# A real-part Fourier transform computed on folded halves, with one rotation table and one weight tile built or loaded at another place

## Chip, cores, metric

The kernel runs on one core of a Trainium2 chip. The time is device microseconds (us) of one execution; several executions are made and their median is quoted.

## What is computed

The program computes two transformer-like blocks over 1,024 positions of width 1,024. The change lies in the mixer of the first block. There a projection of the normalised input gives u (384 columns, a state-space mixer), f (256 columns, a Fourier mixer) and q, k, v (windowed attention). The Fourier mixer and the recurrence of the state-space mixer, cut to what matters:

```python
def fourier_mixer(f, w_fft):            # f: (1, 1024, 256), 4 heads of 64
    ff = f.astype(jnp.float32).reshape(bsz, seq, FFT_HEADS, HEAD_DIM)
    mixed = jnp.fft.fft2(ff, axes=(1, 3), norm='ortho').real.astype(f.dtype)
    return jnp.einsum('bshd,hde->bshe', mixed, w_fft).reshape(bsz, seq, FFT_WIDTH)
...
    lam_bar = jnp.exp(lam * dt)         # complex, 2 directions x 24 groups x 64 states
    _, h_dir = lax.associative_scan(_scan_combine, (a, bu), reverse=rev, axis=1)
```

Only the real part of the two-dimensional transform is kept. With A = f times the cosine matrix of the head dimension and B = f times minus the sine matrix (both already multiplied by `w_fft`), the result over positions is cos(2 pi s t / 1024) A plus sin(2 pi s t / 1024) B.

## The kernel before

Everything in this part of the program is written out by hand: each engine has its own list of instructions, semaphores join them, and the order in which an engine's instructions are written is the order in which it runs them. The transfers spoken of here are all issued from one queue, SP's.

**Projection.** Ten units of 128 output columns (`win_units`, lines 168 to 171): units 0 and 1 give f, 2 to 4 give u, 5 to 7 give q, 8 k, 9 v. For unit n, SP loads 512 KB of weights into `win_raw[n % 2]` (`load_unit`), ScalarE (ACT) rounds them to `win_upper` (line 2074), VectorE (DVE) subtracts to get `win_lower` (`split`, line 2296) and TensorE (PE) runs 48 matmuls of 512 columns (`unit_step`, line 2423). ACT then copies the unit from PSUM (line 2078, `z_ready`). PE's unit n waits for `split(n)` on DVE; ACT's `split(n)` waits for the end of unit n - 2; SP's load of unit n waits for `split(n - 2)` on DVE.

**The Toeplitz tile.** Between the loads of units 3 and 4, SP also writes the convolution taps to DRAM (15 transfers, lines 2007 and 2009), waits for them, and reads them back in shifted order into `toep` (8 transfers of 192 KB, line 2012). `toep` is first used by PE after the attention (line 359).

**The mixer's own order.** PE: the product of the head-dimension matrices with `w_fft` (line 251); the head-dimension stage on f, 8 position tiles with 256 moving columns per pair of heads (line 258), copied by ACT into `f_mixed` (line 393); transposes of u (line 267), copied by DVE into `u_rows` (line 457); transposes of `u_rows` (line 275), copied by ACT into `u_chunk` (line 396); transposes of v (line 280); then the transform over positions (line 289): 8 position tiles x cosine and sine x 2 pairs x 2 halves of the output = 64 fp32 matmuls of 512 columns into four PSUM banks, with 16 loads of 512 KB of the transform matrix through four buffers (line 238). ACT copies the four banks into `yc_t` (line 402, `yf_ready`). Only then PE goes on: a loop over 8 blocks with six items of attention each, beginning with `states` (line 305) and `scores` (line 314), while DVE does row maxima, rotation and scans.

**The rotation tables.** `turns(d)` on DVE builds, for each of the two directions, a 128 x 2 x 12 x 128 table of powers by seven doublings. A doubling of width w works on pieces of `step` of the 12 pairs, each piece being four multiplies, a wait, two adds and a wait (lines 477 to 483). Before, both tables are built after the six copies of `u_rows` and after PE's transposes of them (`uc_turned`, 6); the piece is at most 384 elements.

An fp32 matmul on PE shows as two records in the trace, so 64 matmuls are 128 records; a transpose and a matmul of the rounded operands (line 2423) show as one.

## Time and profile before

| | |
|---|---|
| runs of the kernel before | 3650.12, 3654.16, 3656.3 us; median 3654.16 |
| span of the profiled execution | 3651.0 us, 37524 instructions |
| PE busy | 3376.1 us (92%) |
| DVE busy | 1487.4 us (41%) |
| ACT busy | 1020.5 us (28%) |
| GpSimd (POOL) busy | 217.6 us (6%) |
| mean granted TensorE clock | 0.948 of full |
| chain that ended last, by engine | PE 80%, DVE 10%, issue 4%, ACT 4%, ACTq 1% |
| of it line 2423 (projection) and line 289 (transform over positions) | 2% and 2% |

The span runs from the first to the last instruction of one profiled execution. Its own device time is not given apart from the three runs above, so the table sets the span beside the median of the runs: 3.2 us lie between them. Times in the trace are counted from the start of the span. The stage in question lies between 160 and 370 us.

### The profile page before, as it was taken

The page shows a single profiled execution, that of the slowest core. Times are in us where ns is not written, and L with a number is a line of the kernel's source. Part 1 is how long each engine was busy: PE and PEld are TensorE (multiplying, and loading weights), DVE is VectorE, ACT ScalarE, POOL GpSimd, SP SyncE. Part 2 cuts the span into 40 slices and gives each one's busy share as a digit, 9 for nine tenths or more (in the row PEclk, how much of TensorE's full clock was granted, in tenths as well). Part 3 has the DMA queues.
Part 4 walks back from the last instruction along what each step waited for, and adds up shares of the span by engine and source line. Part 5 has one row for each costly group of instructions (what it writes and reads, how often), then busy time and mean ns, then how long its engine had stood idle before and what let it go on. Part 6 is the DMA issues. An engine that isn't in the chain of part 4 may idle for free.

```text
span 3651.0 us, 37524 instructions
## 1 busy us (share of the span) xinstructions
PE 3376.1 (92%) x14497; PEld 2602.1 (71%) x14497; DVE 1487.4 (41%) x2617; ACT 1020.5 (28%) x1475; POOL 217.6 (6%) x251
## 2 busy tenths in 40 slices
PE   6999888979999999999999998967788899999997
PEld 2575456768888788788888886656345688888885
DVE  6523541453433434411112354699642711111355
ACT  1211223343323223312112232314443322111231
POOL 4100110000000000000000000113330000000000
PEclk9899658989999999999999999888899999999998
DMA  8233000421111134311111342111002311111242
GB/s 276 93 57 107 1 7 24 142 66 47 48 50 46 58 98 140 117 48 46 52 46 52 98 140 97 36 35 39 1 1 98 115 52 46 52 46 46 92 141 100
DMA packets 245610, 260.35 MB, mean 71 GB/s; under 512 B 25680, under 2 KB 187464, under 8 KB 245396
## 3 DMA queue, kind: packets, MB, share of 16 engines
q1 hardware_dynamic: 235736, 253.05, 22.2%
q10 hardware_dynamic: 9788, 6.16, 0.6%
q8 instruction: 53, 0.87, 0.1%
q14 instruction: 33, 0.27, 0.0%
HBM read 237.55 MB, written 21.34 MB: 71 GB/s over the span
## 4 chain that ended last, share of the span: by engine, by line
PE 80%; DVE 10%; issue 4%; ACT 4%; ACTq 1%; DMA 0%; SPq 0%; DVEq 0%; POOL 0%
PE psum L925 39%; PE psum L780 24%; PE psum L2394 2%; PE psum L2423 2%; PE psum L1645 2%; DVE count_junk L1848 2%; PE psum L289 2%; PE psum L314 1%; PE psum L1545 1%; PE psum L333 1%; PE psum L1625 1%; PE psum L362 1%; DVE p L1913 1%; ACT probs L410 1%; PE psum L1635 1%
## 5 line engine op out<-in xcount | busy, mean ns | idle before, releaser
L925 PE MATMUL psum<-x_hi,split_hi 128*128 128x512 f32 x2112 | 662.1, 391 | 15.1 <-DVE x_lo L1197 15.1
L925 PE MATMUL psum<-x_lo,split_hi 128*128 128x512 f32 x2112 | 660.6, 390 | 0.0
L925 PE MATMUL psum<-x_hi,split_lo 128*128 128x512 f32 x2112 | 660.5, 390 | 0.0
L925 PEld LDWEIGHTS psum<-x_hi,split_hi 128*128 128x128 f32 x2112 | 398.3, 189 | 99.9 <-DVE x_lo L1197 17.0
L925 PEld LDWEIGHTS psum<-x_lo,split_hi 128*128 128x128 f32 x2112 | 398.4, 189 | 82.9
L925 PEld LDWEIGHTS psum<-x_hi,split_lo 128*128 128x128 f32 x2112 | 398.0, 188 | 82.9
L780 PE MATMUL psum<-split_hi,src_hi 128*128 128x512 f32 x1312 | 407.0, 392 | 19.6 <-DVE split_lo L750 12.4
L780 PE MATMUL psum<-split_lo,src_hi 128*128 128x512 f32 x1312 | 405.4, 390 | 0.0
L780 PE MATMUL psum<-split_hi,src_lo 128*128 128x512 f32 x1312 | 405.4, 390 | 0.0
L831 DVE TENSOR_TENSOR split_lo<-raw,split_hi 128x1024 fp32r<-128x1024 f32 x132 | 160.9, 1221 | 564.7 <-ACT split_hi L827 564.7
L827 ACT CAST split_hi<-raw 128x1024 fp32r<-128x1024 f32 x132 | 138.7, 1052 | 604.4 <-PE psum L925 595.8
L780 PEld LDWEIGHTS psum<-split_hi,src_hi 128*128 128x128 f32 x1312 | 246.5, 189 | 75.8 <-DVE split_lo L750 15.6
L780 PEld LDWEIGHTS psum<-split_hi,src_lo 128*128 128x128 f32 x1312 | 247.1, 188 | 51.8
L780 PEld LDWEIGHTS psum<-split_lo,src_hi 128*128 128x128 f32 x1312 | 247.1, 188 | 51.6
L749 DVE TENSOR_TENSOR src_lo<-hidden,src_hi 128x512 fp32r<-128x512 f32 x132 | 91.4, 692 | 418.9 <-ACT split_hi L743 418.9
L741 ACT CAST src_hi<-hidden 128x512 fp32r (+1 forms) x132 | 82.1, 622 | 501.7 <-PE psum L780 451.6
L750 DVE TENSOR_TENSOR split_lo<-raw,split_hi 128x1024 fp32r<-128x1024 f32 x164 | 199.8, 1218 | 0.0
L899 DVE TENSOR_TENSOR hidden<-gate,psum 128x1024 f32 (+1 forms) x44 | 53.7, 1221 | 339.7 <-PE psum L925 339.7
L743 ACT CAST split_hi<-raw 128x1024 fp32r<-128x1024 f32 x164 | 171.5, 1045 | 3.4 <-DMA raw<-in_w_out 3.4
L1936 POOL TENSOR_TENSOR split_lo<-raw,split_hi 128x1024 fp32r<-128x1024 f32 (+1 forms) x16 | 37.3, 2333 | 1861.5 <-ACT split_hi L1502 1861.5
L827 ACT ACT_TABLE_LOAD x30 | 38.5, 1283 | 271.7 <-PE psum L925 271.7
L884 DVE SCALAR_TENSOR_TENSOR gate<-psum,conv_now,gate 128x1023 f32<-128x1023 f32 x44 | 56.3, 1279 | 138.1 <-ACT gate L852 138.1
(393 smaller groups left out, 3693.1 us busy)
## 6 DMA issues: line engine op xcount, KB each, us to landing
raw<-in_ffn_w SPq DMA_DIRECT2D x176, 512.0 KB, 3.6
ada_w<-in_w_ada SPq DMA_DIRECT2D x12, 2048.0 KB
raw<-in_w_up SPq DMA_DIRECT2D x44, 512.0 KB, 3.8
raw<-in_w_down SPq DMA_DIRECT2D x44, 512.0 KB, 3.5
raw<-in_w_out SPq DMA_DIRECT2D x32, 512.0 KB, 3.5
res_dram<-hidden SPq DMA_DIRECT2D x32, 512.0 KB, 4.1
hidden<-res_dram SPq DMA_DIRECT2D x32, 512.0 KB, 5.2
dft_w<-in_dft SPq DMA_DIRECT2D x16, 512.0 KB, 3.6
```

The costliest lines, as they stand in the source:

```text
L289: ins = t.matmul(bank(2 * pair + half), f_mixed[:, n, pair, cs, :], dft_w[i % 4][:, HALF * half:HALF * (half + 1)], start=(i == 0), stop=( ...
L741: s.copy(src_hi[slot][:], st.src[:, kk, HALF * half:HALF * (half + 1)])
L743: s.copy(split_hi[slot][:], raw[slot][:]).then_inc(w_hi, 1)
L749: v.tensor_tensor(src_lo[slot][:], st.src[:, kk, HALF * half:HALF * (half + 1)], src_hi[slot][:], ALU.subtract)
L750: v.tensor_tensor(split_lo[slot][:], raw[slot][:], split_hi[slot][:], ALU.subtract).then_inc(w_lo, 1)
L780: ins = t.matmul(bank(2 * n + c), l[slot][:, rows], r[slot][:, HALF * c:HALF * (c + 1)], start=(first and m == 0), stop=(last and m == 2))
L827: nc.scalar.copy(split_hi[u][:], raw[u][:]).then_inc(w_hi, 1)
L831: nc.vector.tensor_tensor(split_lo[u][:], raw[u][:], split_hi[u][:], ALU.subtract).then_inc(w_lo, 1)
L925: ins = t.matmul(bank(4 * par + 2 * u + half), l[u][:, cols], r[:, k, HALF * half:HALF * (half + 1)], start=(k == 0 and m == 0), stop=(k = ...
L1645: ins = t.matmul(bank(6), lat[:, k, :], p2_t[:, k].rearrange("p h q -> p (h q)"), start=(k == 0), stop=(k == b))
L1848: v.tensor_scalar(count_junk[j % 2][:, 0:width(b)], keys(b), trial[:, j:j + 1].bitcast(F32), 0.0, ALU.is_ge, ALU.add, counts[:, j:j + 1]). ...
L2394: t.matmul(bank(j % 4), c_bcast[:, k, :], ada_w[j % 3][:, k, :], start=(k == 0), stop=False)
```

## The change

In plain words:

- The transform over positions uses the symmetry of cosine and sine. DVE folds f in place (`fold_fourier`): positions 1 to 511 become f(t) + f(1024 - t), positions 513 to 1023 become the differences f(t) - f(1024 - t) in the order of t. This is done after `split(4)`, with six instructions of 511 elements.
- The head-dimension stage multiplies the sums with the cosine half and the differences with the sine half, 4 tiles instead of 8, with 128 moving columns each, plus one row for position 512 (`f_mid`). The transform over positions then needs 512 x 512 of the matrix: 16 matmuls of 512 columns, two more of 512 columns on the single row `f_mid` with an alternating sign row, and ten with 2 columns for output position 512.
- The even part and the odd part land in different banks. ACT copies the odd part to `yf_odd` and one column to `yc_t`; DVE writes the sum to `yc_t[0:512]` and the difference, backwards, to `yc_t[513:1024]`.
- The transform matrix is loaded with 4 transfers of 512 KB and two tiny ones (2 KB, and 8 bytes for each of 128 partitions).
- `turns(0)` is run by DVE after `split(5)`, in pieces of at most 256 elements, `turns(1)` right after the six `u_rows` copies.
- `toep` moves to another place in SBUF and is loaded after all projection weights, after the transform matrix and the attention bias, behind `uc_turned`, 6.
- PE's first position matmul also waits for the last copy of `u_chunk` (bank 6 is written).

The diff, cut to its core:

```diff
-    toep = place("toep", [P, CH, GROUPS * GC], RR + 16 * KB)
+    toep = place("toep", [P, CH, GROUPS * GC], RR)
...
-    turn = [place("turn", [P, 2, PAIRS, NCH], RR)[:], carry[1][:, :, :, 0:NCH]]
+    turn = [place("turn", [P, 2, PAIRS, NCH], RR + 16 * KB)[:], carry[1][:, :, :, 0:NCH]]
...
         sp.wait_ge(win_mm, Z_ALL)
-        for i in range(2 * NT):
-            if i >= 4:
-                sp.wait_ge(dft_mm, i - 3)
-            sp.dma_start(dft_w[i % 4][:], a["dft"][P * (i // 2):P * (i // 2 + 1), i % 2, :]).then_inc(dft_in[i % 4], 16)
+        for i in range(4):
+            sp.dma_start(dft_w[i][:], a["dft"][P * i:P * (i + 1)]).then_inc(dft_in[i // 2], 16)
+        sp.dma_start(dft_alt[:], a["dft_alt"]).then_inc(dft_in[1], 16)
+        sp.dma_start(dft_alt_cols[:], a["dft_alt_cols"]).then_inc(dft_in[1], 16)
         sp.wait_ge(u_turned, 6)
         sp.dma_start(att_bias[:], a["att_bias"]).then_inc(bias_in, 16)
+        sp.wait_ge(uc_turned, 6)
+        for s in range(CH):
+            sp.dma_start(toep[GC * s:GC * (s + 1), :, :],
+                         toep_dram[7 - s:15 - s].rearrange("t c n -> c t n")).then_inc(toep_in, 16)
...
         pe.wait_ge(fw_ready, 1)
-        for n in range(NT):
+        pe.wait_ge(f_folded, 1)
+        for n in range(4):
             if n >= 2:
                 pe.wait_ge(fm_ready, n - 1)
             for pair in range(2):
-                ins = t.matmul(bank(4 + n % 2, 2 * P, 2 * P * pair), f_t[:, pair, P * n:P * (n + 1)],
-                               fw[:, pair].rearrange("p c e -> p (c e)"), start=True, stop=True)
+                for cs in range(2):
+                    at_n = HALF * cs + P * n
+                    ins = t.matmul(bank(4 + n % 2, P, P * (2 * pair + cs)), f_t[:, pair, at_n:at_n + P], fw[:, pair, cs, :],
+                                   start=True, stop=True)
             ins.then_inc(fm_mm, 1)
+        pe.wait_ge(fm_ready, 3)
+        for pair in range(2):
+            ins = t.matmul(bank(4, P, P * pair)[0:1], f_t[:, pair, HALF:HALF + 1], fw[:, pair, 0, :], start=True, stop=True)
+        ins.then_inc(fm_mm, 1)
...
-        pe.wait_ge(fm_ready, NT)
-        for i in range(2 * NT):
-            n, cs = i // 2, i % 2
-            pe.wait_ge(dft_in[i % 4], 16 * (i // 4 + 1))
+        pe.wait_ge(uc_ready, 6)
+        for n in range(4):
+            if n % 2 == 0:
+                pe.wait_ge(dft_in[n // 2], 64 if n else 32)
             for pair in range(2):
-                for half in range(2):
-                    ins = t.matmul(bank(2 * pair + half), f_mixed[:, n, pair, cs, :], dft_w[i % 4][:, HALF * half:HALF * (half + 1)],
-                                   start=(i == 0), stop=(i == 2 * NT - 1))
-            ins.then_inc(dft_mm, 1)
-        pe.wait_ge(yf_ready, 4)
+                for cs in range(2):
+                    t.matmul(bank(2 * pair + cs), f_mixed[:, n, pair, cs, :], dft_w[n][:, cs, :],
+                             start=(n == 0), stop=(n == 3 and cs == 1))
+        for pair in range(2):
+            t.matmul(bank(2 * pair), f_mid[:, pair, :], dft_alt[:], start=False, stop=True)
+        for pair in range(2):
+            for n in range(4):
+                t.matmul(bank(6, 2, 2 * pair), f_mixed[:, n, pair, 0, :], dft_alt_cols[:], start=(n == 0), stop=False)
+            ins = t.matmul(bank(6, 2, 2 * pair), f_mid[:, pair, :], dft_alt_cols[0:1, :], start=False, stop=True)
+        ins.then_inc(dft_mm, 1)
+        pe.wait_ge(yf_ready, 3)
...
-        act.wait_ge(dft_mm, 2 * NT)
-        for i in range(4):
-            s.copy(yc_t[:, 3 + i // 2, HALF * (i % 2):HALF * (i % 2 + 1)], bank(i)).then_inc(yf_ready, 1)
+        act.wait_ge(dft_mm, 1)
+        for pair in range(2):
+            s.copy(yf_odd[:, pair, :], bank(2 * pair + 1)).then_inc(yf_odd_ready, 1)
+        s.copy(yc_t[:, 3:5, HALF:HALF + 1], bank(6, 4).rearrange("p (a c) -> p a c", a=2)[:, :, 0:1]).then_inc(yf_ready, 1)
...
-                step = min(PAIRS, 3 * NCH // w)
+            step = max(x for x in (3, 4, 6, PAIRS) if x * w <= (3 if d else 2) * NCH)
...
+    def fold_fourier(dve, v, steps):
+
+        dve.wait_ge(z_ready, Z_F)
+        for pair in range(2):
+            low, high, back = f_t[:, pair, 1:HALF], f_t[:, pair, HALF + 1:SEQ], f_t[:, pair, HALF + 1:SEQ][:, ::-1]
+            steps.add(v.tensor_tensor(f_diff[:, 1:HALF], low, back, ALU.subtract))
+            steps.settle()
+            steps.add(v.tensor_tensor(low, low, back, ALU.add))
+            steps.settle()
+            steps.add(v.tensor_copy(high, f_diff[:, 1:HALF]))
+            steps.settle()
+        dve.sem_inc(f_folded, 1)
...
-        dve.wait_ge(uc_turned, 6)
-        for d in range(2):
-            turns(d)
+        turns(v, steps, 1)
         steps.add(v.tensor_scalar(sink_neg[:], sink_row[:], -1.0, None, ALU.mult))
-        dve.wait_ge(yf_ready, 4)
+        for pair in range(2):
+            dve.wait_ge(yf_odd_ready, pair + 1)
+            even, odd = bank(2 * pair), yf_odd[:, pair, :]
+            steps.add(v.tensor_tensor(yc_t[:, 3 + pair, 0:HALF], even, odd, ALU.add))
+            ins = v.tensor_tensor(yc_t[:, 3 + pair, HALF + 1:SEQ][:, ::-1], even[:, 1:HALF], odd[:, 1:HALF], ALU.subtract)
+            ins.then_inc(yf_ready, 1)
...
-        sp.wait_ge(k_in_dram, 16 * 15)
-        for s in range(CH):
-            sp.dma_start(toep[GC * s:GC * (s + 1), :, :],
-                         toep_dram[7 - s:15 - s].rearrange("t c n -> c t n")).then_inc(toep_in, 16)
         for n in range(4, len(win_units)):
             sp.wait_ge(win_lo, n - 1)
             load_unit(n)
+        sp.wait_ge(k_in_dram, 16 * 15)
         mix_sync(sp)
...
         for n in range(3, len(win_units)):
             split(n)
+            if n == 4:
+                fold_fourier(dve, v, steps)
+            elif n == 5:
+                turns(v, steps, 0)
```

How the instructions stand on SP's queue around the load of projection unit 4 (the buffers `win_raw_96` and `win_raw_97` are `win_raw[0]` and `win_raw[1]`; the last two rows are of unit 4 and of the first half of unit 5). Before:

```order
L2009 DMA toep_dram<-k_sum 16x384
L2012 DMA toep<-toep_dram 16x8x384 [waits k_in_dram]
L2012 DMA toep<-toep_dram 16x8x384 x7
L1992 DMA win_raw_96<-in_w_in 128x8x128 [waits win_lo]
L1992 DMA win_raw_97<-in_w_in 128x8x64 [waits win_lo]
```

In the changed kernel:

```order
L2049 DMA toep_dram<-k_sum 16x384
L2032 DMA win_raw_96<-in_w_in 128x8x128 [waits win_lo]
L2032 DMA win_raw_97<-in_w_in 128x8x64 [waits win_lo]
```

The wait for the taps in DRAM and the eight reads of `toep` have left the place ahead of unit 4's weights.

DVE between the splits of units 4 and 5 in the changed kernel (`win_lower_100` and `win_lower_101` are `win_lower[0]` and `win_lower[1]`; before, the two splits stand next to each other and nothing stands between the splits of units 5 and 6 either):

```order
L2333 TENSOR_TENSOR win_lower_100<-win_raw_96,win_upper_98 128x1024 [waits win_hi]
L505 TENSOR_TENSOR f_diff<-f_t 128x511 [waits z_ready]
L507 TENSOR_TENSOR f_t<-f_t 128x511 [waits dve_steps]
L509 COPY f_t<-f_diff 128x511 [waits dve_steps]
L505 TENSOR_TENSOR f_diff<-f_t 128x511 [waits dve_steps]
L507 TENSOR_TENSOR f_t<-f_t 128x511 [waits dve_steps]
L509 COPY f_t<-f_diff 128x511 [waits dve_steps]
L2333 TENSOR_TENSOR win_lower_101<-win_raw_97,win_upper_99 128x1024 [waits dve_steps,win_hi]
```

Behind the last of these rows stand the 62 instructions of `turns(0)`, and behind them the split of unit 6.

PE's transform over positions in the changed kernel, whole (`dft_w_112` to `dft_w_115` are its four buffers); before it is 64 matmuls of the form of the first row:

```order
L307 MATMUL psum<-dft_w_112,f_mixed 128x512 [waits dft_in0,uc_ready]
L307 MATMUL psum<-dft_w_112,f_mixed 128x512 x3
L307 MATMUL psum<-dft_w_113,f_mixed 128x512 x4
L307 MATMUL psum<-dft_w_114,f_mixed 128x512 [waits dft_in1]
L307 MATMUL psum<-dft_w_114,f_mixed 128x512 x3
L307 MATMUL psum<-dft_w_115,f_mixed 128x512 x4
L310 MATMUL psum<-dft_alt,f_mid 128x512 x2
L313 MATMUL psum<-dft_alt_cols,f_mixed 128x2 x4
L314 MATMUL psum<-dft_alt_cols,f_mid 128x2
L313 MATMUL psum<-dft_alt_cols,f_mixed 128x2 x4
L314 MATMUL psum<-dft_alt_cols,f_mid 128x2
```

## Rows read from the trace of the kernel before

**Rows 1.** Chain of waits, 203 to 291 us: start, length, what.

```profile
203.46 1.60 DMA toep_dram<-k_sum
...
210.06 11.39 DMA win_raw<-in_w_in
221.52 1.05 ACT win_upper L2074
223.88 67.02 PE psum L2423 x288
```

**Rows 2.** Chain of waits, 293 to 370 us.

```profile
293.88 7.41 PE psum L258 x32
...
310.79 54.95 PE psum L289 x128
365.76 2.06 ACT yc_t L402 x4
367.87 1.53 PE psum L305 x24
```

**Rows 3.** Timeline of PE and DVE: start, length, engine, line, tiles, count, idle before.

```profile
218.86 0.61 PE L2423 MATMUL psum<-x_hi,win_lower 128*128 128x512 f32 x2
223.88 1.22 PE L2423 MATMUL psum<-x_hi,win_upper 128*128 128x512 f32 x2 [4.40 <-DVE win_lower L2296]
...
248.49 1.23 DVE L2296 TENSOR_TENSOR win_lower<-win_raw,win_upper 128x1024 fp32r<-128x1024 f32 x1 [9.65 <-ACT win_upper L2074]
259.37 1.22 DVE L2296 TENSOR_TENSOR win_lower<-win_raw,win_upper 128x1024 fp32r<-128x1024 f32 x1 [9.65 <-ACT win_upper L2074]
```

**Rows 4.** Timeline of DVE, 184 to 326 us: a 512-element operation, then the tables.

```profile
184.42 0.69 DVE L2305 TENSOR_TENSOR x_lo<-h_tmp,x_hi 128x512 fp32r<-128x512 f32 x1
...
310.00 0.07 DVE L463 MEMSET turn<- 128x12 f32 x1 [3.94 <-PE psum L275]
...
313.91 0.36 DVE L477 TENSOR_TENSOR turn_tmp<-turn,pw 128x192 f32<-128x192 f32 x1
...
315.77 0.56 DVE L477 TENSOR_TENSOR turn_tmp<-turn,pw 128x384 f32<-128x384 f32 x1
...
318.83 0.56 DVE L477 TENSOR_TENSOR turn_tmp<-turn,pw 128x384 f32<-128x384 f32 x1
...
325.00 0.07 DVE L463 MEMSET carry<- 128x12 f32 x1
```

**Rows 5.** PE's head-dimension product and two small kinds of matmul, by line, then timeline.

```profile
L251 PE MATMUL psum<-fw_rows,dft_d x8: 275/275/348, 292.1 to 292.9; 128*128 128x128 f32 x8
L2395 PE MATMUL psum<-ada_b,ones_row x24: 587/640/692, 40.8 to 151.2; 1*128 1x512 f32 x24
L2406 PE MATMUL psum<-c_pad,lam_b x96: 276/401/402, 114.9 to 132.6; 128*128 128x32 f32 x96
```

**Rows 6.** Busy time by stretch (PE, PEld, DVE, ACT, POOL with records; granted clock; DMA share; GB/s).

```profile
116.00:118.00 2.00, 2.00 (x19) 2.00 (x18) 2.00 (x5) 0.00 (x0) 0.00 (x0) 0.95 0.97 252
118.00:120.00 2.00, 2.00 (x11) 2.00 (x11) 1.93 (x7) 0.00 (x0) 0.00 (x0) 0.50 0.20 51
...
301.00:306.00 5.00, 3.79 (x26) 3.05 (x24) 3.81 (x6) 0.64 (x2) 0.00 (x0) 1.00 0.01 3
306.00:311.00 5.00, 4.46 (x33) 3.67 (x34) 0.95 (x11) 3.69 (x8) 0.00 (x0) 1.00 0.00 0
```

**Rows 7.** Timeline of PE behind the transform: scores, then the second `states`.

```profile
370.69 1.04 PE L314 MATMUL psum<-k_t,q_t 64*128 64x256 f32 x4 [0.24 <-DVE att_max L537]
371.91 1.13 PE L314 MATMUL psum<-k_t,q_t 64*128 64x256 f32 x4 [0.18 <-DVE att_max L537]
...
375.88 2.83 PE L305 MATMUL psum<-u_chunk,state_in 128*64 128x128 f32 x24 [2.84 <-DVEq L498]
```

**Rows 8.** Timeline of DVE: six scans forward (block 0), six backward (block 7).

```profile
377.55 2.82 DVE L514 TENSOR_TENSOR_SCAN rot<-prm,rot 128x128 f32<-128x128 f32 x6
...
558.85 2.82 DVE L514 TENSOR_TENSOR_SCAN rot<-prm,rot 128x128 f32<-128x128 f32 x6
```

More of the change, by code:

```diff
@@ L180, in body @@
     fw = place("fw", [P, 2, 2, P], RR + 42 * KB)
-    f_mixed = place("f_mixed", [P, NT, 2, 2, P], XR + 32 * KB)
-    dft_w = [place(f"dft_w{i}", [P, SEQ], XR + 4 * KB * i) for i in range(4)]
+    f_mixed = place("f_mixed", [P, 4, 2, 2, P], XR + 32 * KB)
+    f_mid = place("f_mid", [1, 2, P], XR + 40 * KB)
+    dft_w = [place(f"dft_w{i}", [P, 2, HALF], XR + 4 * KB * i) for i in range(4)]
+    dft_alt = place("dft_alt", [1, HALF], XR + 16 * KB)
+    dft_alt_cols = place("dft_alt_cols", [P, 2], XR + 18 * KB)
+    yf_odd = place("yf_odd", [P, 2, HALF], XR + 28 * KB)
+    f_diff = place("f_diff", [P, HALF], RR + 10 * KB)
     u_rows = place("u_rows", [P, GROUPS, CH, GC], RR)
@@ L390, in mix_scalar @@
         s.copy(fw[:].rearrange("p a c e -> p (a c e)"), bank(2)).then_inc(fw_ready, 1)
-        for n in range(NT):
+        for n in range(4):
             act.wait_ge(fm_mm, n + 1)
             s.copy(f_mixed[:, n].rearrange("p a c e -> p (a c e)"), bank(4 + n % 2)).then_inc(fm_ready, 1)
+        act.wait_ge(fm_mm, 5)
+        s.copy(f_mid[:].rearrange("o a e -> o (a e)"), bank(4, 2 * P)[0:1]).then_inc(fm_ready, 1)
         for i in range(6):
@@ L2474, in constants @@
         "dft": dft.astype(np.float32),
+        "dft_alt": alternate[None, :].astype(np.float32),
+        "dft_alt_cols": np.repeat(alternate[0:P, None], 2, 1).astype(np.float32),
         "dft_d": dft_d.astype(np.float32),
```

57 lines of the change are left out of this document (29 added, 28 removed).

## Prediction

> **What bounds the kernel now.** I read the chain of waits first: PE has 80% of it and the whole span is a sequence of stages, so a stage is worth what PE, or whoever PE waits for, takes in it. Then I followed the chain through the stage that the change touches. The reader should see three things there. First, a hole: the last tap transfer ends at 205.06, the eight reads of `toep` and then unit 4's weights follow, these take 11.39 us to land, are rounded by ACT (1.05), split by DVE (1.23), and only then PE begins unit 4 at 223.88 [rows 1, 3]. PE had ended unit 3 at about 218.86 + 0.45 = 219.31, since pairs of its matmuls start 0.45 us apart, and was idle 4.4 us [rows 3]. Second, the transform over positions is 128 records in 54.95 us, on PE alone, 0.859 us for each of 64 matmuls [rows 2]. Third, DVE is not on the path there: it begins the tables at 310.00 after 3.94 us idle, the first takes until 325.00, and a second of the same length ends at about 340, while PE multiplies until 365.76 [rows 2, 4].
>
> **The part in the projection.** Unit 4's load no longer stands behind the eight reads of `toep`. It is issued at about 204; even with the 11.39 us it takes now, and 1.05 + 1.23 for rounding and split, its weights are ready at 217.7, before PE's 219.31. So the hole closes. What comes back is more than the hole: six units of 10.88 us (two splits that each follow a unit stand 10.88 apart [rows 3]) are 65.28 us, and they took 67.02 [rows 1], 1.74 us more, at the start of which a pair took 1.22 instead of 0.61 [rows 3]. The projection ends at 219.31 + 65.28 = 284.59 instead of 290.90: **6.3 us less**.
>
> What DVE gets in exchange must fit. The fold: six operations, none longer than the 0.69 us of a 512-element subtraction [rows 4], 4.1 us with their waits somewhat more. The split of unit 4 can now be done when unit 2 has ended (two units before 230.19, that is 208.43, plus 1.05 and 1.23: 210.7), so the fold ends by 215.5. The next split is wanted only when unit 3 has ended and ACT has rounded, 220.4. Cost nothing; its cover is 5 us. Then `turns(0)`: up to width 8 as now, 310.00 to 313.91, 3.9 us; width 16 is one piece of 192, 1.86; a piece of 384 takes 3.06 [rows 4]. Now there are two pieces of 192 for width 32 (3.72) and three of 256 for width 64 (between the two, 2.26 each, 6.78): 16.3 us instead of 15.0. It runs from 221.7 to 238.0, and only then comes the split of unit 6, done at 239.3. PE wants it at 219.31 + 2 x 10.88 = 241.07. Cost nothing, with only **1.8 us** to spare; behind that split stand SP's load of unit 8 and nothing else that is wanted before 250. The wait for the taps that is now ahead of the mixer's loads has long been satisfied.
>
> **Head-dimension stage.** Now 16 matmuls of 256 columns from 293.88 until the u transposes, 7.0 us of the 7.41 that include the last one's end [rows 2]. After: 16 matmuls of 128 columns in four groups, at the pace of line 251 (8 records from 292.1 to 292.9, 0.115 each [rows 5]) 0.9 us a group, with the same copies between the groups, then two of one row: about 4.2 us. **2.8 us less** (2.3 to 3.3). The transposes and copies up to the transform keep their durations; DVE's table 1 starts right after the `u_rows` copies, 3.9 us earlier against them than table 0 did. The added wait for the last `u_chunk` copy falls together with PE's v transposes: nothing.
>
> **Transform over positions.** 16 matmuls, and two of 512 columns on a single row. The nearest rows for a single row are the bias matmuls, 640 ns a record, not shorter than 592 to 600 for full ones [rows 5]; I charge them in full: 18 x 0.859 = 15.5 us. Ten matmuls with 2 columns, 20 records: no row has so few. 128 x 32 records came 19 in 2 us, 0.105 each, at full clock and 11 in 2 us, 0.18, at half [rows 6]; records of a 64-column weight 24 in 1.53 us, 0.064 [rows 2]. I take 0.105, the full-size weight at full clock: 2.1 us (1.3 to 3.6). Together 17.6 instead of 54.95: **37.4 us less**. The Trainium skill, "TensorE: Matmul & The Clock Gate", section "Back-to-back issue gap", gives about 60 cycles, 25 ns, for 1 to 64 columns; by it the tail would be 0.5 us and the sum 1.6 us lower. The rows with 32 columns disagree.
>
> Transfers: 12 loads of 512 KB vanish; four remain and are issued at the end of the projection as now, 17 us ahead of their use. Two tiny ones, the bias (wanted by the first row maximum, over 20 us after the u transposes that release it) and `toep` (over 200 us) follow; the slowest load above took 11.39 us. Nothing.
>
> **Behind it.** Now four ACT copies, 2.1 us until `states` [rows 2]. After: one copy (0.6), then four DVE operations of about 0.65 us, one of which waits for the second copy without losing: 3.2 us, **1.1 us more** (0.6 to 2.5). DVE has finished table 1 15 us after the `u_rows` copies, PE's transform ends 22 us after them (they end at 306.06, it starts at 310.79 [rows 2, 4] and lasts 17.6): table 1 stays hidden by 7 us.
>
> **Clock.** PE is granted 2.4 GHz all through here. When it ran only 32-column matmuls from 114.9, the granted clock fell to 1.2 GHz at 117.9 [rows 6]; after the idle 4.4 us it was low too [rows 3]. After the change PE does 2.1 us of 2-column matmuls and then waits 3.2 us. I expect the clock to be at 1.2 when `states` and the first scores run. `states` then takes 2.83 instead of 1.53 [rows 2, 7]; three pairs of scores, 1.22 us apart now [rows 7], lose about 0.6 each: **3.0 us more**. Lower end 0 (the clock holds), upper end 5.0 (each pair doubles). Behind that, the clock is at 1.2 before as well.
>
> **Sum.** -6.3 - 2.8 - 37.4 + 1.1 + 3.0 = -42.4 us. Against the span of 3651.0 this is 3608.6; the median of the runs stands 3.2 us above the span, and I carry that: **3611.8 us**. About 0.2% (7 us) is what a measurement of this kernel can tell from no change.
>
> **Rivals.**
>
> - *The clock holds* through the tail and the wait: 3608.8. For it: the 2.1 us idle at 365.76 now did not lower it for the first `states` (1.53) [rows 2]. Chance 0.18.
> - *Table 0 is late* for unit 6. If `turns(0)` takes over 1.8 us longer than 16.3, PE stops; each us more is one us, and a stop of some length brings the slow restart of 1.74. At 3 us longer: 1.2 + 1.74, 3614.7. Against it: all durations are known. Chance 0.08.
> - *Transposes let the clock fall.* The dense stretch ahead of 56 records of transposes shrinks from 7 to 4 us. The trace had 1.00 all through 301 to 311 [rows 6]. Should it fall, the transposes (about 0.05 us each) and the start of the transform (1.74) give 4.7 us: 3616.5. The rule in "TensorE: Matmul & The Clock Gate" of the Trainium skill, part 4, is that transpose-mode work does not count as busy in the same way; by it this could happen, and the trace of before speaks against it. Chance 0.07.
> - *Moving `toep` doesn't do what it says*: the 11.39 us are unit 4's own and the load runs slower still beside the tap writes. The hole returns only from 13 us on. 3618. Chance 0.03.
> - *The attention stage gives back or takes* a few us, as the granted clock falls at other moments: 3604 to 3622. Chance 0.10.
> - *Slower than before: backward walks.* Four operations of the fold and two behind the transform read or write f32 with a step of minus one. If each cost r us more, two lie on the path, and the four of the fold push the split of unit 6 by 4r less 5 and 1.8 us of slack: 6r - 6.8. From r = 8.2 us (13 times 0.69) the gain of 42.4 is gone; at 10 it is 3665. Against it: backward scans take the same 2.82 us as forward ones [rows 8]. Chance 0.02.
>
> **Numbers.** The forecast has 0.52, the two small rivals beside it are within a few us. The unknown terms (tail, clock, copies, head stage) give 3607 to 3617, the runs scatter by 3 us, and the clock cases reach 3604 and 3618: range 3603 to 3620. Faster: all but the backward walk and an unnamed mishap, 0.96; within 0.2%: 0.02; slower: 0.02.
>
> **What would show it.** PE in line 2423 without the 4.4 us idle, the last unit ending near 284.6; DVE's split of unit 6 ending before PE wants it; 36 records of 512 columns and 20 of 2 in about 17.6 us; PE's wait behind them 3.2 us, for DVE; `states` at 2.8 us; DVE idle before its first of the four operations. I am wrong if PE waits for `win_lower` at unit 6, if DVE is still in table 1 when the transform ends, or if the tail takes much more than 2 us.

## Result and the profile after

| | before | changed |
|---|---|---|
| runs of the first comparison, us | 3650.12, 3651.21, 3654.16, 3656.3 | 3608.9, 3610.46, 3610.54, 3613.01 |
| median | 3652.68 | 3610.5 |
| ratio, 95% interval | | 0.989, 0.9872 to 0.9909 |
| span of the profiled execution | 3651.0 | 3611.2 |
| PE busy | 3376.1 | 3342.4 |
| DVE busy | 1487.4 | 1494.6 |
| mean granted TensorE clock | 0.948 | 0.945 |

The changed kernel is 42 us faster by the medians and 39.8 by the spans; 3611.8 was forecast. The chain of waits of the changed kernel, where [rows 1] and [rows 2] show it before (start, length, what):

```profile
199.82 85.92 PE psum L2464 x379
285.76 1.02 ACT v_t L2115
286.92 1.15 PE psum L262 x8
288.08 0.59 ACT fw L413
288.72 3.89 PE psum L272 x32
292.61 0.53 PE psum L277 x4
...
302.83 13.80 PE psum L307 x32
316.64 1.91 PE psum L310 x4
318.55 0.98 PE psum L313 x8
319.53 0.31 PE psum L314 x2
319.84 1.37 PE psum L313 x8
321.21 0.53 PE psum L314 x2
321.76 0.59 ACT yf_odd L427
322.38 0.69 DVE yc_t L599
323.07 0.60 DVE yc_t L600
323.66 0.60 DVE yc_t L599
324.26 0.61 DVE yc_t L600
324.91 2.83 PE psum L328 x24
```

No load and no `win_lower` stands between PE's matmuls of the projection any more. (`...` stands for lines left out.) The transform runs from 302.83 to 321.74, 18.9 us against 54.95, its last 3.2 us in the ten 2-column matmuls; then ACT and DVE, 3.15 us, and `states` at 2.83.

DVE's timeline of the changed kernel, around the fold and table 0:

```profile
210.69 1.22 DVE L2333 TENSOR_TENSOR win_lower<-win_raw,win_upper 128x1024 fp32r<-128x1024 f32 x1 [9.65 <-ACT win_upper L2111]
211.83 0.68 DVE L505 TENSOR_TENSOR f_diff<-f_t 128x511 f32<-128x511 f32 x1
212.55 0.69 DVE L507 TENSOR_TENSOR f_t<-f_t 128x511 f32<-128x511 f32 x1
...
215.19 0.43 DVE L509 COPY f_t<-f_diff 128x511 f32<-128x511 f32 x1
221.57 1.23 DVE L2333 TENSOR_TENSOR win_lower<-win_raw,win_upper 128x1024 fp32r<-128x1024 f32 x1 [5.96 <-ACT win_upper L2111]
...
238.57 0.42 DVE L497 TENSOR_TENSOR turn<-turn_tmp,turn_tmp 128x256 f32<-128x256 f32 x1
239.02 1.22 DVE L2333 TENSOR_TENSOR win_lower<-win_raw,win_upper 128x1024 fp32r<-128x1024 f32 x1
```

The fold leaves 5.96 us idle behind it (a cover of 5 was reckoned), and operands read backwards cost no more than others. The split of unit 6 ends at 240.24 without an idle time ahead of it. ACT's timeline has the end of unit 5, when PE wants that split:

```profile
242.24 1.05 ACT L2111 CAST win_upper<-win_raw 128x1024 fp32r<-128x1024 f32 x1 [8.92 <-PE psum L2464]
```

This rounding waits for the same end of unit 5. By the 0.1 us that such a rounding starts behind it, unit 5 ended at about 242.14, so 1.9 us were to spare (1.8 forecast).

To compare profiles with each other, one table holds what the following sections use. All times are us: from PE's first projection matmul (line 2423) to the first `states` (line 305), and to the first exponential (line 410); start of the index scores of the second block (line 1545, fp32 matmuls on 64 rows; "first start" of the line); how long these take (first to last start); from there to the end of the span; the span; and median and extremes of the timed runs. The kernels are described below. Each row up to the span is one profiled execution.

| kernel | to `states` | to first exp | index scores at | take | rest | span | runs |
|---|---|---|---|---|---|---|---|
| before | 202.1 | 208.1 | 2290.2 | 40.2 | 1320.6 | 3651.0 | 3652.7 (3650 to 3656) |
| before again | 203.8 | 212.7 | 2295.8 | 30.4 | 1318.3 | 3644.5 | 3651.5 (3640 to 3658) |
| toep only | 195.8 | 201.8 | 2283.8 | 47.1 | 1320.7 | 3651.6 | 3653.6 (3644 to 3657) |
| toep only again | 197.2 | 203.3 | 2283.2 | 30.4 | 1318.2 | 3631.8 | 3646.3 (3633 to 3652) |
| fold only | 175.6 | 184.9 | 2265.5 | 40.9 | 1319.6 | 3626.0 | 3626.8 (3616 to 3629) |
| tables late | 169.0 | 176.9 | 2260.3 | 40.4 | 1320.5 | 3621.2 | 3620.9 (3611 to 3631) |
| changed | 158.2 | 167.6 | 2250.6 | 40.5 | 1320.1 | 3611.2 | 3610.5 (3609 to 3613) |
| changed again | 158.6 | 166.5 | 2251.0 | 40.6 | 1320.1 | 3611.7 | 3607.9 (3600 to 3613) |
| table 0 longer | 166.1 | 173.9 | 2255.1 | 40.8 | 1317.6 | 3613.5 | 3609.9 (3604 to 3615) |
| no small matmuls | 155.0 | 164.4 | 2249.9 | 40.5 | 1320.3 | 3610.7 | 3606.7 (3604 to 3612) |
| small ones first | 158.8 | 166.7 | 2249.1 | 30.4 | 1318.2 | 3597.7 | 3600.0 (3600 to 3615) |
| all narrow first | 160.3 | 169.6 | 2251.0 | 40.5 | 1320.1 | 3611.6 | 3613.0 (3611 to 3614) |
| small first, states early | 156.4 | 165.2 | 2247.1 | 40.8 | 1319.7 | 3607.6 | 3606.4 (3602 to 3610) |
| states early | 155.9 | 163.6 | 2247.9 | 40.4 | 1320.3 | 3608.6 | 3607.1 (3598 to 3610) |

The way up to the first matmul of the head-dimension stage is not the same in every profile. It takes 128.1 and 129.8 us in the two profiles of before, 121.8 and 123.2 in those of toep only, 129.7 with folding alone, and 122.0 to 123.3 in the kernels that fold and load `toep` late (128.9 in table 0 longer, where PE waits). Why profiles of one kernel differ by 1 to 1.7 us there, no run shows. So what is changed behind that point is read more surely from there:

| kernel | head stage to `states` | to first exp | to index scores |
|---|---|---|---|
| before, before again | 74.0, 74.0 | 80.0, 82.9 | 1996.3, 1999.8 |
| toep only, again | 74.0, 74.0 | 80.0, 80.1 | 1997.1, 1995.5 |
| fold only | 45.9 | 55.2 | 1970.9 |
| tables late | 45.9 | 53.8 | 1973.0 |
| changed, changed again | 36.2, 35.6 | 45.6, 43.5 | 1961.9, 1963.1 |
| small first, states early | 34.4 | 43.2 | 1958.8 |
| states early | 32.6 | 40.3 | 1959.7 |

### The profile page after: what moved, and what is told of

Same layout as the page of the kernel before. It is cut to its first block, busy times and chain, and to the rows that moved or that the text cites. A ratio compares the mean times of both kernels' runs of the same rounds, so it can differ in the third digit from the quotient of the medians.

```text
span 3611.2 us, 37400 instructions
## 1 busy us (share of the span) xinstructions
PE 3342.4 (93%) x14429; PEld 2588.7 (72%) x14429; DVE 1494.6 (41%) x2639; ACT 1017.3 (28%) x1471; POOL 217.7 (6%) x251
## 4 chain that ended last, share of the span: by engine, by line
PE 83%; DVE 9%; ACT 4%; issue 3%; ACTq 1%; DVEq 0%; POOL 0%; DMA 0%
PE psum L965 39%; PE psum L820 24%; PE psum L2464 3%; PE psum L2435 2%; PE psum L1531 2%; PE psum L1685 2%; PE psum L337 1%; DVE count_junk L1888 1%; PE psum L1585 1%; PE psum L356 1%; PE psum L1665 1%; PE psum L385 1%; DVE p L1953 1%; PE psum L1675 1%; PE psum L346 1%
## 5 line engine op out<-in xcount | busy, mean ns | idle before, releaser
L820 PEld LDWEIGHTS psum<-split_hi,src_hi 128*128 128x128 f32 x1312 | 246.5, 189 | 75.7 <-DVE split_lo L790 15.6
```

What stands on the lines that cost most here:

```text
L820: ins = t.matmul(bank(2 * n + c), l[slot][:, rows], r[slot][:, HALF * c:HALF * (c + 1)], start=(first and m == 0), stop=(last and m == 2))
```

## Experiments

### The parts, one by one

**toep only.** The kernel before, with the reads of `toep` moved:

```diff
-        sp.wait_ge(k_in_dram, 16 * 15)
-        for s in range(CH):
-            sp.dma_start(toep[GC * s:GC * (s + 1), :, :],
-                         toep_dram[7 - s:15 - s].rearrange("t c n -> c t n")).then_inc(toep_in, 16)
         for n in range(4, len(win_units)):
             sp.wait_ge(win_lo, n - 1)
             load_unit(n)
+        sp.wait_ge(k_in_dram, 16 * 15)
...
         sp.dma_start(att_bias[:], a["att_bias"]).then_inc(bias_in, 16)
+        for s in range(CH):
+            sp.dma_start(toep[GC * s:GC * (s + 1), :, :],
+                         toep_dram[7 - s:15 - s].rearrange("t c n -> c t n")).then_inc(toep_in, 16)
```

> The kernel before with one edit: the eight reads of toep are issued behind all projection weights and the attention bias. My theory: the projection's share of the gain is wholly this edit, so the 4.4 us hole of PE in the projection closes, the slow restart behind it goes, and the time is 6.1 to 6.3 us below the kernel before (about 3646.5), with nothing else moved. Rival A: unit 4's weights are slow by themselves (11.39 us to land), so part of the hole stays: less than 3 us gained. Rival B: toep now loads beside the transform matrix and costs PE something there: the position matmuls no longer take 54.95 us but more.

The stage did what was expected: 6.3 us earlier at `states` (195.8 against 202.1), no hole in the projection, the transform as long as before. The load of unit 4 (issues of SP from 195 to 225 us: size, time to landing), in the kernel before and in toep only:

```profile
win_raw<-in_w_in SPq DMA_DIRECT2D x1, 512.0 KB, 11.4
win_raw<-in_w_in SPq DMA_DIRECT2D x1, 512.0 KB, 4.1
```

So the 11.39 us were those of the load behind the eight reads, and not its own: rival A fell. The time did not follow: 3653.6 against 3653.0 for the kernel before beside it, ratio 0.9999 (0.9986 to 1.0012). By the first table 6.4 us are still there when the index scores of the second block begin, 2,000 us later, and 7 us are lost inside them. This was no rival of mine. The busy time by stretch there (PE, PEld, DVE, ACT, POOL with records; granted clock; DMA share; GB/s), kernel before:

```profile
2290.00:2300.00 10.00, 9.09 (x29) 4.54 (x29) 4.24 (x9) 5.83 (x9) 0.00 (x0) 1.00 0.17 47
2300.00:2310.00 10.00, 9.09 (x27) 4.57 (x26) 6.93 (x8) 5.53 (x8) 0.00 (x0) 0.96 0.00 0
2310.00:2320.00 10.00, 8.89 (x14) 4.06 (x14) 4.22 (x5) 3.13 (x4) 0.00 (x0) 0.50 0.00 1
2320.00:2331.00 11.00, 11.00 (x17) 4.76 (x15) 3.89 (x5) 3.03 (x4) 0.00 (x0) 0.50 0.00 0
```

toep only, the same stage:

```profile
2284.00:2294.00 10.00, 9.09 (x26) 4.34 (x26) 4.11 (x9) 5.82 (x9) 0.00 (x0) 1.00 0.14 42
2294.00:2304.00 10.00, 9.39 (x17) 4.35 (x15) 3.80 (x4) 3.00 (x4) 0.00 (x0) 0.52 0.00 0
2304.00:2314.00 10.00, 9.49 (x14) 4.59 (x15) 4.47 (x5) 2.95 (x5) 0.00 (x0) 0.50 0.00 1
2314.00:2324.00 10.00, 8.89 (x15) 4.09 (x14) 3.95 (x5) 3.62 (x5) 0.00 (x0) 0.50 0.00 0
2324.00:2331.00 7.00, 7.00 (x11) 3.00 (x9) 2.82 (x3) 1.73 (x2) 0.00 (x0) 0.50 0.00 0
```

PE is 89 to 100% busy in both. At the upper clock 26 to 29 records fit into 10 us, at the lower 14 or 15. The clock fell to 1.2 GHz 20 us into the stage in the one and 10 us into it in the other.

**Is that the edit or the execution?** Both kernels were run again, unchanged.

> The toep-only kernel once more. In its first profile the 7 us were still there at the start of the index scores (fp32 matmuls on 64 rows in the second block) and were gone behind them: they took 47.1 us against 40.2 in the kernel before, with the granted clock falling after 10 us instead of 20. My theory now: where the clock falls in that stage differs between executions of one kernel, whatever was edited, so the span less that stage's duration is the measure: 3604.5 for the first profile against 3610.8 before. Expected: span less that stage 3604 to 3605 again, whatever the stage takes. Rival: the shift of 6 us itself puts the stage at a bad moment; then it takes 47 us again and the time stays at 3652 to 3654.

> The kernel before, profiled once more. By the theory of the index scores: span less the duration of that stage is 3610.8 again (within 2 us), while the stage itself may take 30, 40 or 47 us; the timed runs fall in groups about 10 us apart. Rival: the stage takes 40.2 us again and the runs scatter by 3 us only.

Both found the stage at full clock to its end. The line's matmul row (shortest, median and longest duration in ns, then first and last start). Before, first profile:

```profile
L1545 PE MATMUL psum<-ki_t,qi_t x80: 269/589/1220, 2290.2 to 2330.4; 64*128 64x512 f32 x48, 64*128 64x384 f32 x16, 64*128 64x128 f32 x8, 64*128 64x256 f32 x8
```

Before, second profile:

```profile
L1545 PE MATMUL psum<-ki_t,qi_t x80: 269/589/693, 2295.8 to 2326.2; 64*128 64x512 f32 x48, 64*128 64x384 f32 x16, 64*128 64x128 f32 x8, 64*128 64x256 f32 x8
```

toep only, first profile:

```profile
L1548 PE MATMUL psum<-ki_t,qi_t x80: 269/844/1220, 2283.8 to 2330.9; 64*128 64x512 f32 x48, 64*128 64x384 f32 x16, 64*128 64x128 f32 x8, 64*128 64x256 f32 x8
```

toep only, second profile:

```profile
L1548 PE MATMUL psum<-ki_t,qi_t x80: 269/589/693, 2283.2 to 2313.6; 64*128 64x512 f32 x48, 64*128 64x384 f32 x16, 64*128 64x128 f32 x8, 64*128 64x256 f32 x8
```

The same kernel takes 30.4 or 40.2 us there, and another 30.4 or 47.1. So it is not the edit. That it differs from execution to execution, and not only from chip to chip (toep only was profiled on two chips), the timed runs make likely: the twelve runs of toep only again, on one chip, fall into four of 3633 to 3636 us with a mean granted clock of 0.948 to 0.951, and eight of 3645 to 3652 with 0.943 to 0.947. Two profiles of one kernel on one chip were not taken. The rival, that the shift of 6 us brings the stage into a bad moment, fell: the second toep-only profile begins the stage at 2283.2, as the first did at 2283.8, and has 30.4. The median of the twelve, 3646.3, is 6.6 us below the 3652.9 of the kernel before beside them, as first expected of this edit, but the interval of the ratio (0.997 to 1.0002) still holds no change.

My measure, the span less this stage, was not exact: 3601.4 against 3604.5 for toep only, 3614.1 against 3610.8 for before. The rest behind the stage is 2.3 and 2.5 us shorter in the second profiles. Before again is 1.7 us later than before when the head-dimension stage begins, and loses 2.9 more from `states` to the first exponential. The start of the index scores is no exact measure either: 2290.2 and 2295.8 for before, 2283.8 and 2283.2 for toep only, so that the means are 9.5 us apart. At `states` it is 6.45 us between the same means, and all of it lies ahead of the head-dimension stage.

**Tables late**: the changed kernel with

```diff
-            halves = turn_tmp[d]
-            step = max(x for x in (3, 4, 6, PAIRS) if x * w <= (3 if d else 2) * NCH)
+            halves = turn_tmp[1]
+            step = max(x for x in (3, 4, 6, PAIRS) if x * w <= 3 * NCH)
...
+        dve.wait_ge(uc_turned, 6)
+        turns(v, steps, 0)
         turns(v, steps, 1)
...
-            elif n == 5:
-                turns(v, steps, 0)
```

> The changed kernel with both tables built behind the u_rows transposes, in the pieces of before; folding and toep stay changed. My theory: DVE is then the bound behind the transform: tables from 302.0 to 332.0 on the changed kernel's time, the four operations until 334.5, so states starts 9.6 us later than in the changed kernel and the time is 9 to 10 us above it (about 3620). Rival: there is enough room beside PE's work or the wait is hidden in the attention's first block: under 3 us.

**Fold only**: the same, and `toep` at its old place and time, so that only the folding is left of the change:

```diff
-    toep = place("toep", [P, CH, GROUPS * GC], RR)
+    toep = place("toep", [P, CH, GROUPS * GC], RR + 16 * KB)
...
-    turn = [place("turn", [P, 2, PAIRS, NCH], RR + 16 * KB)[:], carry[1][:, :, :, 0:NCH]]
+    turn = [place("turn", [P, 2, PAIRS, NCH], RR)[:], carry[1][:, :, :, 0:NCH]]
...
-        sp.wait_ge(uc_turned, 6)
-        for s in range(CH):
-            sp.dma_start(toep[GC * s:GC * (s + 1), :, :],
-                         toep_dram[7 - s:15 - s].rearrange("t c n -> c t n")).then_inc(toep_in, 16)
...
+        sp.wait_ge(k_in_dram, 16 * 15)
+        for s in range(CH):
+            sp.dma_start(toep[GC * s:GC * (s + 1), :, :],
+                         toep_dram[7 - s:15 - s].rearrange("t c n -> c t n")).then_inc(toep_in, 16)
         for n in range(4, len(win_units)):
```

> Folding alone: toep is read early again, both tables are built late. If the parts add up: span less index scores is that of the kernel with late tables (3580.8) plus 6.3 = 3587.1, that is 23.7 below the kernel before, so folding gains 23.7 alone and 33.5 with the table out of the way. Rival: the parts depend on each other, e.g. the hole in the projection costs nothing once DVE is the bound behind it; then under 3 us between the two.

From the head-dimension stage to `states` the kernel before takes 74.0 us, folding alone 45.9, with or without the early reads of `toep`, and the changed kernel 36.2 (35.6 in its second profile). So folding alone is worth 28.1 us and the move of table 0 9.7 (9.6 was forecast) to 10.3. With both tables behind the transposes PE waits 13.5 us for DVE behind the transform (11.6 with folding alone) instead of 3.2. The parts add up, the rival of under 3 us between the two kernels fell: moving `toep` is worth 6.3 to 6.6 us at `states` without folding (either pair of profiles) and 6.6 with it (175.6 against 169.0, one profile each). By the measure that the expectation names, span less index scores, it is 3585.1 against 3580.8, that is 4.3 for 6.3 expected, and folding alone gains 25.7 against the first profile of before; that measure was seen above to move by 3 us between two profiles of one kernel. The times agree with the price of the late tables: 3620.9 against 3610.5.

**Table 0 longer**: twelve copies of 512 elements behind `turns(0)`.

```diff
             elif n == 5:
                 turns(v, steps, 0)
+                for _ in range(6):
+                    steps.add(v.tensor_copy(f_diff[:], turn[0][:, 0].rearrange("p a b -> p (a b)")[:, 0:HALF]))
+                    steps.settle()
+                    steps.add(v.tensor_copy(f_diff[:], turn[0][:, 1].rearrange("p a b -> p (a b)")[:, 0:HALF]))
+                    steps.settle()
```

> The changed kernel with twelve more 512-element copies on DVE behind table 0, about 5.6 us (12 x 0.47). My theory: the split of unit 6 had 1.95 us to spare, so PE waits 3.7 us for it at unit 6; with a clock that is low at the restart it costs up to 1.7 more: 3.7 to 5.4 us above the changed kernel. Rival: the cover is larger than I read it (ACT or the loads set unit 6): under 1 us. What also is asked: whether an idle time of 3.7 us is followed by the slow restart that 4.4 us was followed by.

PE's timeline in that kernel:

```profile
240.93 0.61 PE L2469 MATMUL psum<-x_hi,win_lower 128*128 128x512 f32 x2
245.21 0.73 PE L2469 MATMUL psum<-x_hi,win_upper 128*128 128x512 f32 x2 [3.67 <-DVE win_lower L2333]
245.78 0.94 PE L2469 MATMUL psum<-x_lo,win_upper 128*128 128x512 f32 x2
246.53 1.05 PE L2469 MATMUL psum<-x_hi,win_lower 128*128 128x512 f32 x2
```

The wait is 3.67 us for 3.7 expected, and the restart is slow, so the cover of 1.9 us is shown and so is what lies beyond it. `states` came 7.7 us later than in the changed kernel (mean of its two profiles), for at most 5.4 expected. The rest of it is a second fall of the clock, in the head-dimension stage:

```profile
294.00:296.00 2.00, 2.00 (x11) 2.00 (x11) 0.00 (x0) 0.23 (x1) 0.00 (x0) 0.50 0.84 299
```

From the start of that stage to the transform it took 15.6 us against 14.0 in both profiles of the changed kernel; 1.6 us went there. It was ahead of the transposes, with the clock at 1.00 again when they ran. No other profile shows it, and no run shows why it came. The time did not show the delay: 3609.9, in two groups of three runs, 3604 to 3606 and 3614 to 3615. The delay had shrunk to 4.3 us at the index scores; the first block's gated matmuls (line 381) took 15.1 us from first to last start against 17.4 and 17.6 in the changed kernel. A loss of this size can be read from the trace, not from a few runs.

### What lowers the clock ahead of `states`

Three edits of the changed kernel, and the changed kernel again. Without the small matmuls:

```diff
-        for pair in range(2):
-            for n in range(4):
-                t.matmul(bank(6, 2, 2 * pair), f_mixed[:, n, pair, 0, :], dft_alt_cols[:], start=(n == 0), stop=False)
-            ins = t.matmul(bank(6, 2, 2 * pair), f_mid[:, pair, :], dft_alt_cols[0:1, :], start=False, stop=True)
```

> The changed kernel without the ten 2-column matmuls; output position 512 of the Fourier mixer is then not computed (stale values are copied). Theory T1: the clock falls because of the small matmuls (it fell at 320.4, inside them, 1.3 us before PE began to wait), so without them states (2.83) is back at 1.53 and the scores at 1.22 a pair: 3.2 (tail) + 1.3 + 2.0 = 6.5 us below the changed kernel. Theory T2: what counts is the whole weak stretch with the two single-row matmuls and the 3.2 us wait; then only the tail's own 3.2 us go, perhaps 2.1 at full clock, and states stays at 2.83. T3: the clock falls later, after states: 4.5 to 5 us.

With them ahead of the 16 dense ones:

```diff
+        pe.wait_ge(dft_in[1], 64)
+        for pair in range(2):
+            for n in range(4):
+                t.matmul(bank(6, 2, 2 * pair), f_mixed[:, n, pair, 0, :], dft_alt_cols[:], start=(n == 0), stop=False)
+            t.matmul(bank(6, 2, 2 * pair), f_mid[:, pair, :], dft_alt_cols[0:1, :], start=False, stop=True)
         for n in range(4):
             if n % 2 == 0:
...
-        for pair in range(2):
-            for n in range(4):
-                t.matmul(bank(6, 2, 2 * pair), f_mixed[:, n, pair, 0, :], dft_alt_cols[:], start=(n == 0), stop=False)
-            ins = t.matmul(bank(6, 2, 2 * pair), f_mid[:, pair, :], dft_alt_cols[0:1, :], start=False, stop=True)
```

> The changed kernel with the ten 2-column matmuls ahead of the position matmuls instead of behind them; the two single-row matmuls stay last. T1 (the small matmuls lower the clock): the clock may fall early, at the start of the dense matmuls, cost up to 1.7 us there, or not at all since they are short; it is full at states: 1.3 + 2.0 + about 0.9 (small ones at full clock) = 4.2 us gained, at least 2.5. T2 (the weak stretch before states, single-row matmuls and wait): the clock falls still before states, gain only 0.9.

With the two single-row matmuls ahead too:

```diff
+        for pair in range(2):
+            t.matmul(bank(2 * pair), f_mid[:, pair, :], dft_alt[:], start=True, stop=False)
         for n in range(4):
...
-                             start=(n == 0), stop=(n == 3 and cs == 1))
+                                   start=(n == 0 and cs == 1), stop=(n == 3))
-        for pair in range(2):
-            ins = t.matmul(bank(2 * pair), f_mid[:, pair, :], dft_alt[:], start=False, stop=True)
```

> As the former, with the two single-row matmuls ahead too, so that 16 full matmuls run up to the 3.2 us wait. T1: the same as the former, 4.2 us gained. T2: if the single-row matmuls count as weak activity, this one keeps the clock through states and the former doesn't: 4.2 us here against 0.9 there. If both are at half clock in states, the 3.2 us wait alone does it.

And the changed kernel beside them, unedited:

> The changed kernel again, on the chip of the next three, as their reference: 42 us below the kernel before (41 to 43.5), states at 2.83 us, the clock falling inside the ten small matmuls.

The stretches of the changed kernel (columns as above), in its first profile, show the fall inside the small matmuls:

```profile
319.00:320.00 1.00, 1.00 (x9) 0.97 (x9) 0.00 (x0) 0.00 (x0) 0.00 (x0) 1.00 0.00 0
320.00:321.00 1.00, 1.00 (x8) 1.00 (x7) 0.00 (x0) 0.00 (x0) 0.00 (x0) 0.63 0.00 0
321.00:322.00 1.00, 0.72 (x3) 0.62 (x3) 0.00 (x0) 0.24 (x1) 0.00 (x0) 0.50 0.00 0
```

In its second profile it was not so: the small matmuls ran at the upper clock (2.6 us), and the clock fell half a microsecond into the wait. `states` took 2.83 us in all of them, with the small matmuls last, first, or absent, and with dense matmuls right up to the wait. The theory that the small ones alone lower the clock (T1) fell. T2, that the single-row matmuls count with the wait, fits the first two kernels and fell with the third, where dense matmuls up to the wait did not help. What all four share is the wait of 3.19 us, and in the kernel with all narrow ones first it was enough by itself. There the 16 full matmuls ended at 322.1, and the clock fell inside the wait:

```profile
322.00:323.00 1.00, 0.07 (x1) 0.00 (x0) 0.27 (x1) 0.89 (x2) 0.00 (x0) 1.00 0.00 0
323.00:324.00 1.00, 0.00 (x0) 0.00 (x0) 1.00 (x3) 0.98 (x3) 0.00 (x0) 1.00 0.00 0
324.00:325.00 1.00, 0.00 (x0) 0.00 (x0) 1.00 (x3) 0.55 (x1) 0.00 (x0) 0.56 0.00 0
```

Enough, but not needed: the versions of the next section have no such wait, and their clock falls too.

Moving the small ones can have a price: with all narrow ones first, and in the early-states version with the small ones first, the 16 dense matmuls took 15.6 us instead of 13.8, since the clock was at 0.5 for some 3 us near their start. With only the small ones first it was not (13.9), although PE's instructions up to there are the same as in that early-states version. So the same order of work can go either way. Without the small ones the gain at `states` is 3.4 us: about their own time, no more. That the version with the small ones first has the best median of all, 3600.0, is no gain of the edit, for it is at `states` when the changed kernel is (158.8 and 158.4). Its runs are 3599.5, 3599.6 and 3600.0, with a mean granted clock of 0.948, and 3615.1 and 3615.4 with 0.943; the first was profiled, and its index scores took 30.4 us instead of 40.5.

### A version that gains

PE needs not wait for all four banks: `states` writes banks 5 and 6, the first scores banks 0 and 1, the first transposes of probabilities banks 2 and 3.

```diff
-        pe.wait_ge(yf_ready, 3)
+        pe.wait_ge(yf_odd_ready, 1)
...
                     states(i // Q_HEADS)
+                if i == 0:
+                    pe.wait_ge(yf_ready, 1)
                 scores(i)
...
+                if i == DELAY:
+                    pe.wait_ge(yf_ready, 2)
                 turn_probs(i - DELAY)
...
         act.wait_ge(dft_mm, 1)
+        s.copy(yc_t[:, 3:5, HALF:HALF + 1], bank(6, 4).rearrange("p (a c) -> p a c", a=2)[:, :, 0:1]).then_inc(yf_odd_ready, 1)
...
-            dve.wait_ge(yf_odd_ready, pair + 1)
+            dve.wait_ge(yf_odd_ready, pair + 2)
```

Once with the small matmuls first, once with them last:

> A version meant to beat both: small matmuls first; ACT copies the column of position 512 first, PE's states waits for that alone, the first scores for the first pair, the first transposes of probabilities for the second pair. states then starts 0.3 us behind the transform instead of 3.15, and the first maximum comes as soon as DVE has done its four operations. Expected: the first exponential 6.5 to 8.5 us behind the end of the transform instead of 12.5, so 4 to 6 us, and with the tail at full clock up to 7 us, below the changed kernel. If it is under 2 us, DVE (four operations, then maxima) was the bound there and not PE.

> The changed kernel with the small matmuls left last, but PE's states waits only for the copy of the column of position 512, the first scores for the first pair, the first transposes of probabilities for the second pair. The version with the small matmuls first reached the first exponential 43.2 us behind the start of the head-dimension stage, though its clock dipped at the start of the transform (15.6 instead of 13.8 us); the changed kernel needs 45.6 and 43.5 in its two profiles. Expected here: 41 to 42.5 us, span less index scores 3567 to 3569 against 3570.7 and 3571.1, so 2 to 4 us gained. Rival: DVE is the bound there (four operations, six maxima) and PE's early start is worth under 1 us.

The chain of the second (states early, small ones last):

```profile
319.27 0.98 PE psum L313 x8
320.26 0.32 PE psum L314 x2
320.60 0.17 ACT yc_t L430
320.82 2.63 PE psum L328 x24
323.44 1.16 PE psum L337 x2
```

`states` starts 0.24 us behind the last small matmul. It still does not run at the upper clock: the stretches of this kernel show the fall at its start, behind small matmuls at full clock (2.6 us) and no wait to speak of.

```profile
320.00:321.00 1.00, 0.75 (x9) 0.65 (x10) 0.00 (x0) 0.40 (x2) 0.00 (x0) 1.00 0.00 0
321.00:322.00 1.00, 1.00 (x14) 1.00 (x14) 0.72 (x2) 0.98 (x3) 0.00 (x0) 0.53 0.09 16
```

With the small ones first and `states` 0.25 us behind the single-row matmuls, `states` took 2.28 us, the clock falling inside it. So no version here has `states` at 1.53 behind the shortened transform, with the long wait or without it.

The first exponential comes 40.3 us behind the start of the head-dimension stage with the small ones last (45.6 and 43.5 in the changed kernel; 41 to 42.5 expected), the index scores 1959.7 against 1961.9 and 1963.1. That is 2.1 to 3.3 us there, for 2 to 4 expected, from one profile; by the starts of the index scores in the first table it is 2.7 to 3.1. The medians, 3607.1 against 3610.5 and 3607.9, lie that way and do not settle it. The version with the small ones first missed its forecast of 4 to 6 us at the first exponential: 43.2, which is 9.1 us behind the transform for 6.5 to 8.5 expected, since its transform took 1.8 us longer at the lower clock. At the index scores it is 3.1 to 4.3 us ahead of the changed kernel; its median is 3606.4.

## Why the prediction was right, and where it was not

- **The hole in the projection**, -6.3: shown by itself, 6.3 us at `states` in the first pair of profiles and 6.6 in the second. The restart at the lower clock was part of it. The load was reckoned at 11.39 us in its new place too, and took 4.2; nothing hung on it.
- **Fold and table 0 at no cost**, 1.8 us to spare: 1.9 measured; a longer table makes PE wait 3.67 us for 3.7 reckoned. The rival of the late table is the right one to fear and was 1.9 us away.
- **Head-dimension stage**, -2.8: from its start to the first `u_rows` copy 5.10 us (288.72 to 293.82) against 7.89, so 2.79.
- **Transform**, -37.4: measured 18.9 instead of 17.6, -36.0. This is the term that was mis-sized. The dense part was 13.8, as reckoned; the two single-row matmuls took 1.91 for 1.72; the ten small ones 3.2 for 2.1, of which half ran at the lower clock. At full clock they are 2.6, 20 records at 0.13 and not the 0.105 of the 32-column ones. By the 25 ns of the Trainium skill's page "TensorE: Matmul & The Clock Gate", section "Back-to-back issue gap", I had estimated 0.5 us: the trace disagrees.
- **Behind it**, +1.1: 3.15 us for 2.11, +1.04. Writing and reading backwards costs nothing here (0.68 and 0.69 us), the rival on the other side had no ground.
- **Clock**, +3.0: `states` 2.83 as said; to the first exponential 9.36 us for 6.08, +3.3. The effect was right. Its cause, the narrow matmuls with the wait, is in part shown: the wait is enough with dense matmuls right up to it, and behind the narrow ones the clock falls without the wait too. In the second profile of the changed kernel the scores found the upper clock again and it was 7.9 us.
- **Transposes** did not let the clock fall: the granted clock was 1.00 from 293 to 302 us of the changed kernel, while they ran, with only 4.4 us of dense work ahead of them. It was so in the other profiles of kernels that fold as well; in that with table 0 longer the clock had fallen ahead of them and was back at 1.00 while they ran. The rule that I cited from the Trainium skill, "TensorE: Matmul & The Clock Gate", Part 4, had no effect that a profile here shows.
- **The sum**: up to the first exponential 40.5 us were gained (208.1 to 167.6), 42.4 forecast; 1.4 us of the difference are the transform, 0.3 the clock, the rest small terms. From the first to the last instruction of the profiles it is 39.8. The median fell by 42.2. That it meets the forecast to 1.3 us is partly luck. The 3.2 us that I carried from span to median were not the distance of the two: in the runs that have both, the time stands 1.7 to 1.9 us above the span of the same execution, and the rest was scatter between executions. And I had taken "the runs scatter by 3 us" for the noise, from three runs. With more runs one and the same kernel spans 18 us (3640 to 3658), and the prediction has no term for the index scores, where profiles of the same instructions lie 10 to 17 us apart. The "3604 and 3618" of its range do not come out of its clock term either, which at 0 to 5.0 us gives 3608.8 to 3613.8. The range of 3603 to 3620 held for the four runs of the first comparison; of the four later ones of the same kernel one is at 3600.
- **Left open**: what decides when the clock falls in the index scores and ahead of `states`, and why the first attention and the way up to the head-dimension stage scatter by 1 to 3 us. No run separates these.

## To carry to other kernels

Halving both sizes of a dense transform is worth what the engine beside it leaves: here 28.1 us alone, and 9.7 more once the work that lay hidden under the long matmuls was moved elsewhere. Before costing a shortened stage, list what else was hidden under it. Where a gain is under one percent, measure it in the trace, from a point just ahead of the changed stage to one just behind it, and find the stage in which the end time scatters, before believing a median either way.

## What the hardware did that I had not expected

- A stage of fp32 matmuls on 64 rows, PE 89 to 100% busy, ran wholly at 2.4 GHz in three of the profiles compared here and fell to 1.2 GHz after 10 or 20 us in others: 30.4, 40 to 41, or 47.1 us for the same instructions. Two kernels, each profiled twice, differ from themselves by this.
- A wait of 3.19 us ahead of `states` was followed by `states` at 1.2 GHz in all six profiles that have it, with dense matmuls up to the wait in one of them. The wait of 2.14 us ahead of it in the kernel before and in toep only was not in three of four profiles; in the fourth `states` took 2.39 us, so the clock fell inside it. With narrow matmuls somewhere ahead and a wait of only 0.25 us the clock fell inside `states` too (2.63 and 2.28 us).
- f32 operands with a step of minus one: 0.68 and 0.69 us for 511 elements, like 0.69 for 512 forward ones [rows 4].
